# First transfers and first steps put in another order, and the last layer's mixer input left out, in a four-layer transformer kernel on one core

## The reference, cut to what matters

```
for l in range(2):                       # first_block
    h = rms_norm(x, g_mix_norm[l]); z = h @ w_in[l]
    ... attention, spatial gating and pooling of parts of z ...
    x = x + mix @ w_out[l]
    h = rms_norm(x, g_ffn_norm[l])
    x = x + (silu(h @ w_gate[l]) * (h @ w_up[l])) @ w_down[l]
# two blocks of the second kind (gated linear attention, sparse attention),
# with a gate floor from a softmax over hg_lb_2, then the last norm:
return x * rsqrt(mean(x * x) + eps) * final_norm_g_2
```

## Time and profile before

| what | us |
|---|---|
| median of 3 runs | 3233.62 (3229.6 to 3239.56) |
| the profiled execution's own time | 3231.99 |
| its span, first to last instruction | 3230.2 |
| mean granted TensorE clock | 0.986 of full speed |
| TensorE busy | 3130.9 |
| GpSimd busy | 1902.7 |
| VectorE busy | 1492.0 |
| ScalarE busy | 746.2 |

### The profile page before, as it was taken

How to read it: one execution, slowest core, us unless ns; L and a number is a source line. 1 busy time by engine, 2 the same in 40 slices (tenths; PEclk the granted TensorE clock), 3 DMA queues, 4 the chain that set the end, 5 groups by cost and what they waited for, 6 DMA issues and landing times.

```text
span 3230.2 us, 43793 instructions
## 1 busy us (share of the span) xinstructions
PE 3130.9 (97%) x15408; PEld 2512.5 (78%) x15408; DVE 1492.0 (46%) x2578; ACT 746.2 (23%) x1538; POOL 1902.7 (59%) x881
## 2 busy tenths in 40 slices
...
DMA packets 71592, 263.16 MB, mean 81 GB/s; under 512 B 8064, under 2 KB 8064, under 8 KB 71296
## 3 DMA queue, kind: packets, MB, share of 16 engines
...
...
## 4 chain that ended last, share of the span: by engine, by line
PE 62%; POOL 16%; issue 14%; DVE 5%; ACT 2%; POOLq 0%; DVEq 0%; DMA 0%; SPq 0%; ACTq 0%
PE bank L617 61%; POOL w_hi L1360 9%; POOL w_lo L1366 6%; PE bank L1221 1%; DVE rope L1879 1%; DVE arena L1882 1%; DVE arena L2410 0%; ACT arena L1821 0%; DVE arena L2238 0%; DVE rope L1882 0%; DVE arena L2426 0%; DVE arena L1879 0%; PE bank L897 0%; DVE w_lo L2264 0%; ACT act_hi L1489 0%
## 5 line engine op out<-in xcount | busy, mean ns | idle before, releaser
L1360 POOL TENSOR_TENSOR w_hi<-ring,one 128x1024 fp32r<-128x1024 f32 x430 | 820.6, 1908 | 1248.4 <-PE bank L617 1194.9
L1366 POOL TENSOR_TENSOR w_lo<-ring,w_hi 128x1024 fp32r<-128x1024 f32 x422 | 1037.7, 2459 | 33.1
L617 PE MATMUL bank<-h_hi,w_hi 128*128 128x512 f32 x2256 | 896.0, 397 | 4.8 <-DVE h_lo L1906 2.4
L617 PE MATMUL bank<-h_hi,w_lo 128*128 128x512 f32 x2256 | 881.4, 391 | 0.0
L617 PE MATMUL bank<-h_lo,w_hi 128*128 128x512 f32 x2256 | 880.5, 390 | 0.0
L617 PE MATMUL bank<-act_hi,w_hi 128*128 128x512 f32 (+1 forms) x1392 | 513.5, 397 | 11.0 <-DVE act_lo L2116 9.2
L617 PEld LDWEIGHTS bank<-h_hi,w_hi 128*128 128x128 f32 x2256 | 424.4, 188 | 99.4 <-issue 5.5
L617 PEld LDWEIGHTS bank<-h_hi,w_lo 128*128 128x128 f32 x2256 | 423.9, 188 | 91.0
L617 PEld LDWEIGHTS bank<-h_lo,w_hi 128*128 128x128 f32 x2256 | 424.6, 188 | 85.4 <-issue 1.0
L617 PE MATMUL bank<-act_hi,w_lo 128*128 (+1 forms) x1120 | 440.4, 393 | 0.0
L617 PE MATMUL bank<-act_lo,w_hi 128*128 (+1 forms) x1104 | 416.0, 391 | 1.4 <-DVE act_lo L2445 1.4
...
## 6 DMA issues: line engine op xcount, KB each, us to landing
ring<-wstream SPq DMA_DIRECT2D x480, 512.0 KB, 3.5
par<-params SPq DMA_DIRECT2D x5, 656.5 KB, 4.7
x<-xT SPq DMA_DIRECT2D x4, 512.0 KB, 6.7
outT<-h SPq DMA_DIRECT2D x4, 512.0 KB, 2.7
cst<-const ACTq DMA_DIRECT2D x1, 1412.0 KB, 9.3
...
cst<-const SPq DMA_DIRECT2D x1, 24.5 KB, 2.4
```

What stands on the lines that cost most here:

```text
L617: return pe.matmul(out, lhsT, rhs, start=start, stop=stop)
L1360: return po.tensor_tensor(out, a, one.broadcast_to([P, n]), ALU.mult)
L1366: po.tensor_tensor(pair_[1], raw, pair_[0].bitcast(F32), ALU.subtract).then_inc(done.sem, 1)
```

## The change

- **Loads.** SP issues g_in (8 columns, 4 KB) first, then positions and columns, x's first pair, tile 0, x's other pairs, tiles 1 and 2. The rest of the parameters and the tables are issued by ScalarE's queue when x's third pair has landed. ScalarE waits for x's transfers itself.
- **Tile 0 in halves.** GpSimd splits tile 0 of a first-kind mixer in two halves of 512 columns; `dense(0, 0)` starts on the first and waits for the second at block 4. The counts of the two semaphores grow by one.
- **Order at the start.** The exponential comes first on ScalarE. VectorE makes the lower bounds first and the last five angle steps behind the eight low parts. TensorE waits for s_const only behind `dense(2, 2)`.
- **End.** Behind the last layer ScalarE only squares each block as it comes, and VectorE adds square j - 1 behind block j, into bank 0.
- **Loops.** SP, ScalarE and VectorE have the second kind's two layers written out, since the last differs. By the listing VectorE's program grows from 1645 to 2132 instructions, ScalarE's from 1063 to 1208. `squares_added` moves from a mixer's start to the end of the FFN before it, in the same place of VectorE's order.

```
@@ -284,12 +284,12 @@
-        w1_h = signal("mixer_tile_high", 10 + ND)
-        w1_split = signal("mixer_tile_split", 10 + ND)
...
+        w1_h = signal("mixer_tile_high", 11 + ND, 1)
+        w1_split = signal("mixer_tile_split", 11 + ND, 1)
@@ -582,7 +582,7 @@
-                for t in range(mix + 2 * RING):
+                for t in range(RING, mix + 2 * RING):
                     wait_product(t - RING)
                     load(l * per + (base + t), t % RING)
@@ -592,16 +592,32 @@
+            def next_layer(nf, at):
+                for t in range(RING):
+                    sp.wait_ge(*w_split(nf, t - RING + 1))
+                    load(at + t, t)
+            def x_in(j):
+                sp.dma_start(x[:, j:j + 2, :].rearrange("p a t -> p (a t)"), xT[:, j * T:(j + 2) * T])\
+                    .then_inc(s_x0[j // 2], 16)
+            sp.dma_start(par[:, PAR1["g_in"]], params[0, :, PAR1["g_in"]]).then_inc(s_x0[0], 16)
             sp.dma_start(m1["ta"].bitcast(I32), pos).then_inc(s_pos, 16)
             sp.dma_start(cst[:, COLUMNS], const[:, COLUMNS]).then_inc(s_pos, 16)
-            params_in(0)
-            for j in range(0, ND, 2):
-                sp.dma_start(x[:, j:j + 2, :].rearrange("p a t -> p (a t)"), xT[:, j * T:(j + 2) * T])\
-                    .then_inc(s_x0[j // 2], 16)
+            x_in(0)
+            load(0, 0)
+            for j in range(2, ND, 2):
+                x_in(j)
+            load(1, 1)
+            load(2, 2)
             with sp.Fori(0, LAYERS) as l:
                 layer(l, l, 0, PER1, FREE1)
-            with sp.Fori(0, LAYERS) as l:
+                next_layer(l + 1, l * PER1 + PER1)
+            for l in range(LAYERS):
                 layer(l, l + LAYERS, BASE2, PER2, FREE2)
+                if l < LAYERS - 1:
+                    next_layer(l + LAYERS + 1, BASE2 + (l + 1) * PER2)
@@ -768,9 +784,11 @@
                 def dense(g, s):
-                    pe.wait_ge(*w1_split(l, s + 1))
+                    pe.wait_ge(*w1_split(l, s + 1 if g else 0))
                     z_wait(g)
                     for k in range(ND):
+                        if g == 0 and k == ND // 2:
+                            pe.wait_ge(*w1_split(l, 1))
                         if g == 0:
                             pe.wait_ge(*u_ready(l, k + 1))
@@ -810,6 +828,7 @@
                 dense(0, 0)
                 dense(1, 1)
                 dense(2, 2)
+                pe.wait_ge(s_const, 16)
                 pe.wait_ge(*n_ac(2 * l, ND - 2))
                 pe.wait_ge(*n_sq(2 * l, ND))
                 norm_sum(2 * l, (0, ND - 1))
@@ -1337,14 +1356,12 @@
             pe.sem_inc(down_out.sem, down_out.start)
-            pe.wait_ge(s_const, 16)
             with pe.Fori(0, LAYERS) as l:
                 mixer1(l)
                 ffn(l, 2 * l + 1, squares[1])
             with pe.Fori(0, LAYERS) as l:
                 mixer2(l)
                 ffn(l + LAYERS, 2 * l + 5, squares[2])
-            pe.wait_ge(*u_ready(2 * LAYERS, ND))
             pe.wait_ge(*n_ac(8, ND - 2))
             pe.wait_ge(*n_sq(8, ND))
             norm_sum(8, (0, ND - 1))
@@ -1380,7 +1397,15 @@
-                    halves(ring[:, t % RING, :], weights1(s), w1_h, l * w1_h.per + (s + 1), w1_split)
+                    if s == 0:
+                        for n in range(2):
+                            c = slice(n * TILE // 2, (n + 1) * TILE // 2)
+                            times_one(early[0][0][:, c], ring[:, 0, c], TILE // 2).then_inc(w1_h.sem, 1)
+                            po.wait_ge(*w1_h(l, n))
+                            po.tensor_tensor(early[0][1][:, c], ring[:, 0, c], early[0][0][:, c].bitcast(F32),
+                                             ALU.subtract).then_inc(w1_split.sem, 1)
+                    else:
+                        halves(ring[:, t % RING, :], weights1(s), w1_h, l * w1_h.per + (w1_h.start + s + 1), w1_split)
@@ -1477,13 +1502,18 @@
-            def front(n, nf, tables=False):
-                sc.wait_ge(*s_par(nf, 16))
+            def front(n, nf, first=False):
+                if not first:
+                    sc.wait_ge(*s_par(nf, 16))
                 for j in range(ND):
                     g = par[:, PAR1["g_in"]][:, j:j + 1]
-                    sc.wait_ge(*x_ready(n, j + 1))
-                    if tables and j == 2:
+                    if not first:
+                        sc.wait_ge(*x_ready(n, j + 1))
+                    elif j % 2 == 0:
+                        sc.wait_ge(s_x0[j // 2], 16 if j else 32)
+                    if first and j == 4:
+                        sc.dma_start(par[:, ND:NPAR], params[0, :, ND:NPAR]).then_inc(s_par.sem, 16)
                         sc.dma_start(cst[:, TABLES], const[:, TABLES]).then_inc(s_const, 16)
                     sc.activation(bank[j][:, :], x[:, j, :], ACT.Copy, scale=g)
                     sc.activation(u_hi[j], x[:, j, :], ACT.Copy, scale=g).then_inc(u_h.sem, 1)
@@ -1851,23 +1881,25 @@
+            sc.wait_ge(lb_s, 3)
+            sc.activation(lbt[:, 0:8], lbt[:, 0:8], ACT.Exp).then_inc(lb_e, 1)
             front(0, 0, True)
-            sc.wait_ge(s_const, 16)
             sc.wait_ge(s_rope, 9)
             sc.activation(m1["cos"], m1["sin"], ACT.Sin, scale=0.5).then_inc(s_ropea, 1)
             sc.wait_ge(s_ropea, 1)
             sc.activation(m1["sin"], m1["sin"], ACT.Sin).then_inc(s_ropea, 1)
-            sc.wait_ge(lb_s, 3)
-            sc.activation(lbt[:, 0:8], lbt[:, 0:8], ACT.Exp).then_inc(lb_e, 1)
             with sc.Fori(0, LAYERS) as l:
                 mixer1(l)
                 ffn(2 * l + 1, l, par[:, PAR1["g_ffn"]], squares[1])
                 front(2 * l + 2, l + 1)
-            with sc.Fori(0, LAYERS) as l:
+            for l in range(LAYERS):
                 mixer2(l)
                 ffn(2 * l + 5, l + LAYERS, par[:, PAR2["g_ffn"]], squares[2])
-                front(2 * l + 6, l + LAYERS + 1)
+                if l < LAYERS - 1:
+                    front(2 * l + 6, l + LAYERS + 1)
+            for j in range(ND):
+                sc.wait_ge(*x_ready(8, j + 1))
+                sc.activation(usq[:, j, :], x[:, j, :], ACT.Square).then_inc(n_sq.sem, 1)
             norm_std(8)
@@ -1950,9 +1982,14 @@
                     ve.wait_ge(*down_out(nf, j + 1))
                     add(x[:, j, :], x[:, j, :], bank[j][:, :]).then_inc(x_ready.sem, 1)
-                    if j > 0:
+                    if not last and j > 0:
                         front((nf + 1, j - 1))
-                front((nf + 1, ND - 1))
+                    elif last and j > 1:
+                        squares_added(n + 1, usq, bank[0], j - 1)
+                if not last:
+                    front((nf + 1, ND - 1))
+                    for j in range(1, ND - 1):
+                        squares_added(n + 1, usq, bank[5], j)
@@ -1962,8 +1999,6 @@
-                for j in range(1, ND - 1):
-                    squares_added(2 * l, usq, bank[5], j)
@@ -2180,8 +2215,6 @@
             def mixer2(l):
-                for j in range(1, ND - 1):
-                    squares_added(2 * l + 4, usq, bank[5], j)
@@ -2480,36 +2513,11 @@
-            def x_landed(j):
-                ve.wait_ge(s_x0[j // 2], 16)
-                ve.sem_inc(x_ready.sem, 2)
-            step(ve.tensor_copy(pf, m1["ta"].bitcast(I32)))
-            step(ve.tensor_scalar(ang, pf, C("invfreq"), None, ALU.mult))
-            x_landed(0)
-            step(ve.tensor_scalar(turns, ang, 1 / (2 * math.pi), 12582912.0, ALU.mult, ALU.add))
-            step(ve.tensor_scalar(turns, turns, 12582912.0, None, ALU.subtract))
-            x_landed(2)
-            x_landed(4)
-            for part in TWO_PI_PARTS[:2]:
-                step(ve.scalar_tensor_tensor(ang, turns, -part, ang, ALU.mult, ALU.add))
-            x_landed(6)
-            for part in TWO_PI_PARTS[2:]:
-                step(ve.scalar_tensor_tensor(ang, turns, -part, ang, ALU.mult, ALU.add))
-            step(ve.tensor_scalar(ang, ang, 3.1415925, -3.1415925, ALU.min, ALU.max))
-            for j in range(ND):
-                front((0, j))
-            ve.memset(ksl[:, :, :], 0.0)
-            ve.wait_ge(s_const, 16)
...
-            ve.wait_ge(lb_e, 1)
@@ -2517,6 +2525,11 @@
+            step(ve.tensor_copy(pf, m1["ta"].bitcast(I32)))
+            step(ve.tensor_scalar(ang, pf, C("invfreq"), None, ALU.mult))
+            step(ve.tensor_scalar(turns, ang, 1 / (2 * math.pi), 12582912.0, ALU.mult, ALU.add))
+            step(ve.tensor_scalar(turns, turns, 12582912.0, None, ALU.subtract))
+            ve.wait_ge(lb_e, 1)
@@ -2525,18 +2538,27 @@
+            for part in TWO_PI_PARTS[:2]:
+                step(ve.scalar_tensor_tensor(ang, turns, -part, ang, ALU.mult, ALU.add))
+            for j in range(ND):
+                front((0, j))
+            ve.sem_inc(x_ready.sem, ND)
+            for part in TWO_PI_PARTS[2:]:
+                step(ve.scalar_tensor_tensor(ang, turns, -part, ang, ALU.mult, ALU.add))
```

(11 more changed lines are left out.)

6 lines of the change are left out of this document (3 added, 3 removed).

## The result

The changed kernel took 3211.73 us (median of 3 runs, 3211.2 to 3212.74) against 3233.62: ratio 0.9928, 95% interval 0.9913 to 0.9943, so 21.9 us faster. Its profiled execution has a span of 3209.9, which is 20.3 less than before. The forecast was 3217.2 (range 3209 to 3225). TensorE's busy time is 3129.9, within 1 us of the earlier trace rows; what went is standing still.

What follows compares the result with a forecast made beforehand. TensorE, busy 97% of the span, was taken as the bound, with savings mainly where it idles at both ends: 5.4 + 0.7 + 2.0 + 7.6 + 0.2 + 0.5 = 16.4 off 3233.6 gives 3217.2 us, range 3209 to 3225.

Steps and rivals of the forecast that it cites:

- The start: Ahead of the first matmul: TensorE begins at 13.3 us instead of 18.70, 5.4 us saved (4.4 to 6.9).
- the norm sum's wait: At layer 0's norm sum: TensorE's 0.65 us wait for VectorE's square additions goes, 0.7 us saved.
- VectorE becomes the late one: At the start: VectorE's steps, blocked beside GpSimd's splits, give the first low part at 13.3 us and release TensorE.
- the unblocked end: At the start: first low part at 11.8 us if VectorE's angle steps slip through between GpSimd's instructions.
- my bad end: At the start: first low part at 14.3 us if tile 1's split also gets in VectorE's way.
- The doubt about the 32-byte rows: g_in's load at the start: rows below 512 bytes might cost several times its 4 KB; 0.45 us was kept.
- Layer 0's clock: Layer 0's 32 narrow matmuls and the product behind: faster if the clock stays up, 2.0 us taken of 3.3.
- because the idle that distinguishes the two is removed: Layer 0's norm sum: reason given for 2.0 us, as layer 1's same 32 matmuls took 3.63 without an idle ahead.
- The end: Ahead of the last sums: they start at 3207.9 instead of 3215.48, 7.6 us saved (6.9 to 8.1).
- The middle: Between the ends: written-out loops save tens of ns per ScalarE or VectorE step, 0.5 us (0 to 3).
- Rival 1: Whole kernel, everything early: start at 11.8, clocks stay up, written-out loops give 2; 23.6 us saved, 3210; chance 0.15.
- Rival 3: Written-out loops: straight code waits for instruction fetches, ten waits cost 24 us, 3241, slower; chance 0.02.

Runs made afterwards that it cites:

- e12: The change with positions and columns issued by ScalarE's idle queue in place of SyncE's: 3222.6 us (12 runs), ratio 0.9969.
- e1: The kernel before with the new end alone, ScalarE's and VectorE's second-kind loops written out: 3221.97 us (9 runs), ratio 0.9956.
- e4: The changed kernel once more, unaltered: 3212.85 us (6 runs), ratio 0.9938 against before.
- e3: The kernel before with only the second kind's two layers written out on SyncE, ScalarE and VectorE: 3230.5 us (12 runs), ratio 0.9985.

## Why the prediction came out as it did

**The start (5.4 forecast, and 0.7 for the norm sum's wait).** Measured 6.9 at the first matmul and 7.0 at the norm sum, against 6.1 for the two terms together. The prediction's step "VectorE becomes the late one" failed: GpSimd's first half released TensorE. It failed because of the landings. I let tile 0 land at 7.3, 1.3 us behind x's first pair; it landed at 9.2, 2.2 behind it, and x itself at 7.0 and not 6.0. GpSimd therefore began at 9.29 and not at 7.4, and VectorE's last angle step was through at 9.44. The two errors cancel, later bytes but no blocked step, and that the term came out near is luck. The number 11.8 stood in the text as the unblocked end, for a reason (steps slipping between GpSimd's instructions) that did not occur. What the prediction feared is shown by e12: with GpSimd at 7.79 and VectorE 1.5 late, the start is at 18.8, later than the 14.3 of my bad end. The change stands on an edge that neither the diff nor a sum over loads shows. The doubt about the 32-byte rows can go: the Trainium skill's page "DMA: Bandwidth & Descriptors" (Specifications) asks for 512 bytes at least for the full rate, but the 4 KB landed in 1.7 us, sooner than any other load.

**Layer 0's clock (2.0 forecast).** Nothing came in the profile of the change: from the norm sum to a spread in the middle of the mixer (65.18 before, 58.16 after) the change took 27.59 us and before 27.63. The step that failed is "because the idle that distinguishes the two is removed": the idle was gone and the clock fell all the same, and before's second execution, without any change, had the sums in 3.63 and its first spread 1.7 us sooner behind their start. The difference between layer 0 and layer 1 in the earlier trace rows was that in that execution the clock fell in the one and not in the other; in the change's first execution it fell in both. The Trainium skill's page "TensorE: Matmul & The Clock Gate" (the section on why this matters) ties the fall to a long idle. The prediction took from it a sum larger by 3, that is 19.4, which is nearer to the measured 21.9, but not for the page's reason: the clock fell in layer 0 without an idle, and at the end, behind 1.53 us of idle, it stayed up in only three of nine profiles. The page gives no reason for either, so the measurement decides there.

**The end (7.6, and 0.2 for the clock).** Measured 8.24 from VectorE's first addition to the sums (17.24 before, 9.00 after). The step was right, VectorE at one operation each 0.60 instead of my 0.62 to 0.74; the release by the last Square as well. My upper bound of 8.1 held a slip of 0.4: twelve operations of 0.62 from 3199.6 end at 3207.0, not 3207.4, which gives 8.4. Behind it the clock gave 2.4 in the first profile (sums 1.63, spread 0.80) but 0.6 to 0.8 in six of the others. I had valued 2.6 at 0.2; over the nine profiles it is nearer to 1.3.

**The middle (0.5).** Inside its range (0 to 3), for a wrong reason. It is not tens of nanoseconds a step: the waits for ScalarE's copy stayed, 7.3 us in 28 where the earlier trace rows has 7.0. What went is the wait of 1.39 us at the border of the last two layers, which the prediction had not looked at. The other 1.2 us that one pair of profiles shows lie within what one kernel differs from itself.

**The sum.** Located are 7.0 to 7.5 at the start, 8.9 to 10.7 at the end and 1.4 at the border: 17.3 to 19.6, where the medians give 22 to 23. The rest lies in the granted clock, as far as the record shows it. The profiled executions of before took 3231.99 and 3226.25 us at 0.986 and 0.988, its 24 runs beside e1 to e4 3236.4 at 0.9843 on average; the change's three profiles took 3211.5 at 0.9877 on average, its six runs of e4 3214.0 at 0.9865. So before's profiles lie 7.3 us below its runs and the change's 2.5, and the 4.8 between is about what is missing. At half clock half of the time is lost, so a thousandth less of mean clock is 3.2 us of such a span, and the clocks give 8.7 and 3.8, a difference of 4.9 (an estimate from these means). Whether the kernel before falls to half clock more often by its nature, or where, no profile shows. The forecast of 16.4 was short by 0.9 at the start, 0.9 in the middle and 1 to 3 at the end, and long by 2.0 at layer 0's clock. Rival 1 (3210) is nearer to the median, though two of its parts did not happen: no step slipped between GpSimd's instructions, and layer 0's clock did not stay up. Rival 3 is refuted by e3, where straight code cost nothing.
